# A hybrid attention layer on one core: late output weights spread over more attention units, the fourth head's inverse root on VectorE from a bit guess, the root table loaded ahead

## The chip, the core and the metric

The kernel runs on one NeuronCore of one Trainium2 chip. The time is the device time of one execution in microseconds (us). The work of the core is shared by five engines with instruction queues of their own: PE (TensorE, matmuls and transposes), DVE (VectorE), ACT (ScalarE), POOL (GpSimd) and SP, which here only starts transfers. An engine runs its instructions in the order in which they stand; engines wait for one another through semaphores.

## What is computed

One layer over 512 frames and 16 meta tokens of width 1024. The part that the change touches is the token mixer and its output projection:

```python
mu = jnp.mean(o, axis=-1, keepdims=True)                  # retention output, 4 heads of 128
var = jnp.mean(jnp.square(o - mu), axis=-1, keepdims=True)
on = (o - mu) * lax.rsqrt(var + EPS)
ret = jax.nn.silu(g) * on
...
s = jnp.where(sel_ok, q @ k_sel, NEG)                      # sparse attention, 8 heads
att = (softmax(s) @ v_sel) @ w_uv
h = h + jnp.concatenate([ret, att], axis=-1) @ w_out       # the output projection
hn = rmsnorm(h, norm_ffn)
h = h + peer(hn, ...)                                      # 16384 experts, most of the time
```

## The kernel before

The program is a row of blocks with a barrier between them: `project` (input projection and the selection of keys), `mix_rows` (retention, attention, output projection, the norm before the experts and the first two query products), `route` (top experts), `experts`. Matmuls with weights run in three passes over a high and a low part of each operand (`three_pass`), so each piece of a weight is first split: `split_hi` on ACT writes the high part, `split_lo` on POOL subtracts it from the raw weight. The 16 pieces of `w_out` (units 0 to 15 of `ws`) are split inside `mix_rows`; units 0 to 6 early, the rest at steps that the table `LATE_W` gives.

The heart of `mix_rows` is a loop `for i in range(STEPS)` that stands once for each engine. Step `i` treats attention unit `i`, which is one head of one block of 128 rows: 32 units, eight to a block, the widest block (528 keys) first, then 400, 272 and 144 keys. In a step:

- PE computes `scores(i)`, transposes the probabilities of unit `i-2` (`turn_probs`), and multiplies those of unit `i-3` with the values (`values`). At step 9 it also turns the gathered probabilities of the meta keys of the eight units of block 0 (`turn_meta(0)`), at step 11 it adds their part (`add_meta`) and then turns the finished retention columns (`turn_mixed`), which the projection needs. For this last all four heads must be gated.
- DVE computes the masked scores, their peak and the shift (`mask(i)`), and copies the transposed probabilities of unit `i-2` out of PSUM (`copy_probs`). PE's `values(i-3)` waits for that copy.
- ACT computes the exponentials of unit `i`, the high halves of the weights that `LATE_W[i]` names, and at the steps of `NORM_AT` normalizes one retention head.
- POOL copies the meta columns of unit `i`'s probabilities (`meta_probs`), then does the low halves for `LATE_W[i]`, and at the steps of `GATE_AT` multiplies a retention head with its gate. PE's `turn_meta(0)` waits for the copy of unit 7.

Retention's inverse standard deviations are made in two groups: heads 0 to 2 before the loop and head 3 inside it. For head 3 ACT takes the square root at step `LATE_ROOT` = 8, and DVE at step 9 takes the reciprocal and one Newton step (`refine_rstd`, five instructions) and the offset. The square root and the exponential stand in different function tables of ACT, so each change between them is an `ACT_TABLE_LOAD`.

After the loop ACT squares the new rows (`square`), takes their root (`ffn_sqrt`, again behind a table load), DVE refines and scales the rows, PE transposes them (`turn_normed`) and starts on the queries.

## Time and profile before

| | before |
|---|---|
| time, median of 3 runs (lowest, highest) | 1719.62 us (1718.4, 1720.39) |
| the profiled execution: its time, its span | 1721.74 us, 1719.9 us |
| PE, DVE, ACT, POOL busy, share of the span | 98%, 63%, 34%, 55% |
| granted TensorE clock over the span | 0.996 |
| `mix_rows` in the span | about 237 to 391 us |

The span runs from the first to the last instruction of the profiled execution. Times in rows are counted from its start. An instruction's row gives start, duration, engine, line, operation and tiles; what stands in square brackets is the idle time of that engine before it and who ended it.

### The profile page before, as it was taken

How to read it: one execution, taken by the hardware profiler on the slowest of the kernel's cores; microseconds unless marked ns; L12 is line 12 of the kernel's file. 1: busy time of each engine (PE TensorE's matmuls, PEld its weight loads, DVE VectorE, ACT ScalarE, POOL GpSimd, SP SyncE). 2: the span in 40 equal slices, each digit the busy share in tenths (PEclk: the TensorE clock that was granted, in tenths of full speed). 3: DMA queues.
4: the chain of work that ended last, by engine and by line, in shares of the span. 5: the costliest groups of instructions: out<-in, count | busy, mean ns of one | idle time of the engine just before them, and what ended most of it. 6: DMA issues, size and time to landing. Idle time of an engine off the chain costs nothing.

```text
span 1719.9 us, 23334 instructions
## 1 busy us (share of the span) xinstructions
PE 1689.8 (98%) x7786; PEld 1390.4 (81%) x7786; DVE 1090.5 (63%) x2933; ACT 582.0 (34%) x916; POOL 938.8 (55%) x875
## 2 busy tenths in 40 slices
PE   9999999999999999999999999999999999999997
PEld 7867877788888878888888888888888888888886
DVE  4259966455788854444444444434788888888886
ACT  4333217243323222222222222224333333333333
POOL 2744415004433027777777777762777677767710
PEclk9999999999999999999999999999999999999999
DMA  5322131026669544444447444445999999999991
GB/s 176 105 62 60 52 81 60 23 99 221 233 229 309 172 135 147 145 143 143 145 146 248 147 146 143 147 147 190 386 389 368 370 373 367 371 375 367 366 330 49
DMA packets 182673, 351.03 MB, mean 204 GB/s; under 512 B 35600, under 2 KB 118928, under 8 KB 182448
## 3 DMA queue, kind: packets, MB, share of 16 engines
q1 hardware_dynamic: 117824, 255.47, 44.5%
q0 software_dynamic: 34816, 67.41, 11.0%
q10 hardware_dynamic: 29952, 27.28, 4.8%
q8 instruction: 26, 0.43, 0.1%
q14 instruction: 55, 0.45, 0.1%
HBM read 289.04 MB, written 61.02 MB: 204 GB/s over the span
## 4 chain that ended last, share of the span: by engine, by line
PE 63%; DVE 0%; issue 0%; DVEq 0%; ACT 0%
PE psum L240 21%; PE psum L241 21%; PE psum L242 21%; DVE mixed L2135 0%; DVE mixed L2112 0%; DVEq L2059 0%; DVE rstd_final L824 0%; DVE rstd_final L828 0%; DVE rstd_final L822 0%; DVE rstd_final L826 0%; DVE rstd_final L820 0%; ACT rstd_final L2249 0%; DVE rstd_final L2121 0%; DVE rstd_final L2119 0%
## 5 line engine op out<-in xcount | busy, mean ns | idle before, releaser
L2323 POOL DMA_INDIRECT gate_map<-gate_total,gate_at x384 | 403.5, 1051 | 204.9 <-DVE same_expert L2066 114.2
L240 PE MATMUL psum<-x_hi,ts_hi_u 128*128 128x512 f32 x1024 | 399.9, 391 | 4.0 <-PEq L1681 2.2
L241 PE MATMUL psum<-x_lo,ts_hi_u 128*128 128x512 f32 x1024 | 399.1, 390 | 0.0
L242 PE MATMUL psum<-x_hi,ts_lo_u 128*128 128x512 f32 x1024 | 398.9, 390 | 0.0
L1569 DVE TENSOR_TENSOR ts_lo_u<-ts_raw_u,ts_hi_u 128x1024 fp32r<-128x1024 f32 x116 | 142.2, 1226 | 340.7 <-ACT ts_hi_u L1564 338.1
L240 PE MATMUL psum<-v_hi,c_hi 128*128 128x512 f32 x768 | 298.8, 389 | 0.0
L242 PE MATMUL psum<-v_hi,c_lo 128*128 128x512 f32 x768 | 298.8, 389 | 0.0
L241 PE MATMUL psum<-v_lo,c_hi 128*128 128x512 f32 x768 | 298.8, 389 | 0.0
L1564 ACT ACTIVATE ts_hi_u<-ts_raw_u 128x1024 fp32r<-128x1024 f32 x128 | 135.4, 1058 | 398.6 <-PE psum L242 398.6
L2226 ACT ACTIVATE v_hi<-v_raw 128x1024 fp32r<-128x1024 f32 x128 | 135.8, 1061 | 313.3 <-PE psum L242 310.2
L240 PEld LDWEIGHTS psum<-x_hi,ts_hi_u 128*128 128x128 f32 x1024 | 192.6, 188 | 44.7 <-issue 2.6
L242 PEld LDWEIGHTS psum<-x_hi,ts_lo_u 128*128 128x128 f32 x1024 | 192.7, 188 | 40.1
L2311 POOL DMA_INDIRECT sparse_rows<-in_peer_v,v_row x128 | 154.4, 1206 | 129.1 <-DVE sparse_more L2102 38.2
L241 PEld LDWEIGHTS psum<-x_lo,ts_hi_u 128*128 128x128 f32 x1024 | 192.7, 188 | 39.7
L2083 DVE TENSOR_TENSOR v_lo<-v_raw,v_hi 128x1024 fp32r<-128x1024 f32 x128 | 156.8, 1225 | 80.3 <-ACT v_hi L2226 79.9
L2317 POOL DMA_INDIRECT sparse_act<-up_acts_sparse,act_at x128 | 175.3, 1370 | 41.5 <-issue 39.8
L242 PEld LDWEIGHTS psum<-v_hi,c_lo 128*128 128x128 f32 x768 | 144.2, 188 | 30.0
L240 PEld LDWEIGHTS psum<-v_hi,c_hi 128*128 128x128 f32 x768 | 144.2, 188 | 29.8
L241 PEld LDWEIGHTS psum<-v_lo,c_hi 128*128 128x128 f32 x768 | 144.2, 188 | 29.8
L2066 DVE SCALAR_TENSOR_TENSOR same_expert<-expert,gates 128x128 f32<-128x128 f32 x384 | 111.8, 346 | 0.0
L240 PE MATMUL psum<-whi_in,h_hi 128*128 128x512 f32 (+1 forms) x280 | 109.8, 392 | 0.8 <-DVE wlo_in L280 0.8
L1600 ACT ACTIVATE ut_out_u<-psum 128x512 f32<-128x512 f32 x128 | 76.0, 594 | 95.6 <-PE psum L242 94.3
(258 smaller groups left out, 2298.2 us busy)
## 6 DMA issues: line engine op xcount, KB each, us to landing
ts_raw_u<-in_peer_u SPq DMA_DIRECT2D x128, 512.0 KB, 3.6
v_raw<-in_peer_v SPq DMA_DIRECT2D x128, 512.0 KB, 6.0
gate_map<-zeros SPq DMA_DIRECT2D x32, 768.0 KB, 6.6
act_in<-up_acts SPq DMA_DIRECT2D x128, 192.0 KB, 6.3
gate_in<-gate_map SPq DMA_DIRECT2D x128, 192.0 KB, 6.8
up_acts<-ut_out_u ACTq DMA_DIRECT2D x104, 192.0 KB, 1.9
raw_in<-in_w_in SPq DMA_DIRECT2D x56, 256.0 KB, 2.8
ts_raw_wq<-in_peer_wq SPq DMA_DIRECT2D x16, 512.0 KB, 6.3
```

The source lines that it names most:

```text
L240: nc.tensor.matmul(out, l_hi, r_hi, start=first, stop=False)
L241: nc.tensor.matmul(out, l_hi, r_lo, start=False, stop=False)
L242: return nc.tensor.matmul(out, l_lo, r_hi, start=False, stop=last)
L1564: nc.scalar.activation(self.hi[:, n % self.slots], self.raw[:, n % self.raws], ACT.Copy).then_inc(self.hi_done, 1)
L1569: eng_ops.tensor_tensor(self.lo[:, n % self.slots], self.raw[:, n % self.raws], self.hi[:, n % self.slots].bitcast(F32), ALU.subtract).the ...
L1600: nc.scalar.activation(self.out[:, i], self.bank[n % 2], ACT.Gelu).then_inc(self.bank_read, 1)
L2066: nc.vector.scalar_tensor_tensor(out=dn.same[:, j % 2], in0=expert[:, b], scalar=expert[:, b, j:j + 1], in1=gates[:, b].rearrange("p h k - ...
L2083: nc.vector.tensor_tensor(dn.v_lo[:, i], dn.v_raw[:, e % RAW], dn.v_hi[:, i].bitcast(F32), ALU.subtract).then_inc(v_lo_done, 1)
L2226: nc.scalar.activation(dn.v_hi[:, i], dn.v_raw[:, e % RAW], ACT.Copy).then_inc(v_hi_done, 1)
L2311: nc.gpsimd.indirect_dma_start(dn.rows[:, r], None, v_rows, bass.IndirectOffsetOnAxis(places["v_row"][:, j:j + 1], 0)).then_inc(row_in[r], 16)
L2317: nc.gpsimd.indirect_dma_start(dn.picked[:, j:j + 1], None, act_cells, bass.IndirectOffsetOnAxis(places["act_at"][:, j:j + 1], 0)).then_in ...
L2323: nc.gpsimd.indirect_dma_start(gate_cells, bass.IndirectOffsetOnAxis(places["gate_at"][:, b, j:j + 1], 0), dn.total[:, b, j:j + 1], None). ...
```

## The change

1. `LATE_W`: units 9 to 15 of the output weights are split at other steps. Before: 9 and 10 at step 2, then one at each of steps 3 to 7. After: one at each of steps 2, 3, 7, 8, 9, 11 and 12. ACT's high half and POOL's low half move together.
2. Head 3: ACT's square root at step 8 is gone, and with it its two table loads. DVE makes the inverse root by itself from a shift of the bits and three Newton steps: eleven instructions and the offset, twelve in all, at step 7 in place of six at step 9. `LATE_ROOT` is 6, so ACT normalizes head 3 at step 7 (before: 9) and POOL gates it at step 8 (before: 10).
3. Behind the last exponentials ACT runs one unused square root, so the table load for `ffn_sqrt` moves ahead of the squares.
4. In `experts` the loads of activations and gates of one tile signal one semaphore in place of two.

```diff
-    LATE_ROOT = DSA_HEADS
+    LATE_ROOT = DSA_HEADS - 2
     LAST_HEAD, LAST_SUMS = RET_HEADS - 1, 7
-    LATE_W = {1: (7, 8), 2: (9, 10), 3: (11,), 4: (12,), 5: (13,), 6: (14,), 7: (15,)}
+    LATE_W = {1: (7, 8), 2: (9,), 3: (10,), 7: (11,), 8: (12,), 9: (13,), 11: (14,), 12: (15,)}
     NORM_AT = {2: 0, 3: 1, 4: 2, LATE_ROOT + 1: LAST_HEAD}
     GATE_AT = {4: 0, 5: 1, 6: 2, LATE_ROOT + 2: LAST_HEAD}
+    ROOT_BITS, ROOT_STEPS = 0x5F3759DF, 3
...
+            def guessed_roots(y, v, t):
+
+                nc.vector.tensor_scalar(ab["guess"][:], v.bitcast(U32), 1, None, ALU.logical_shift_right).then_inc(guessed, 1)
+                dve.wait_ge(guessed, 1)
+                nc.vector.tensor_scalar(y.bitcast(U32), ab["guess"][:], -1.0, float(ROOT_BITS), ALU.mult, ALU.add).then_inc(guessed, 1)
+                for n in range(ROOT_STEPS):
+                    dve.wait_ge(guessed, 3 * n + 2)
+                    nc.vector.tensor_tensor(t, y, y, ALU.mult).then_inc(guessed, 1)
+                    dve.wait_ge(guessed, 3 * n + 3)
+                    nc.vector.scalar_tensor_tensor(out=t, in0=t, scalar=-0.5, in1=v, op0=ALU.mult, op1=ALU.mult).then_inc(guessed, 1)
+                    dve.wait_ge(guessed, 3 * n + 4)
+                    nc.vector.scalar_tensor_tensor(out=y, in0=t, scalar=1.5, in1=y, op0=ALU.add, op1=ALU.mult).then_inc(guessed, 1)
+                dve.wait_ge(guessed, 3 * ROOT_STEPS + 2)
+
             def inverse_roots(g):
                 hs = HEAD_GROUPS[g]
-                dve.wait_ge(root, g + 1)
-                refine_rstd(nc, dve, refined, g, rstd[:, hs], var[:, hs], ab["ret_step"][:, hs])
+                if g == 0:
+                    dve.wait_ge(root, 1)
+                    refine_rstd(nc, dve, refined, 0, rstd[:, hs], var[:, hs], ab["ret_step"][:, hs])
+                else:
+                    guessed_roots(rstd[:, LAST_HEAD], var[:, LAST_HEAD], ab["ret_step"][:, LAST_HEAD])
...
-                if i == LATE_ROOT:
-                    ret_sqrt(1)
...
+                if i == UNITS - 1:
+                    nc.scalar.activation(ab["unused"][:], ident[:, 0:1], ACT.Sqrt)
...
-                dve.wait_ge(act_in[i], 16 * use)
-                dve.wait_ge(gate_in[i], 16 * use)
+                dve.wait_ge(factors_in[i], 32 * use)
```

What stands on DVE around step 7, before: `mask(7)`, `copy_probs(5)`, `mask(8)`, `copy_probs(6)`.

```order
L1291 ISA att_masked,att_peak<-psum,sel_bias 128x528 [waits att_exp_done,att_scored]
L1291 ISA att_peak 128x1
L1295 TENSOR_SCALAR att_shift<-att_peak 128x1 [waits att_mask_done]
L1302 COPY att_probs_t<-psum 128x512 [waits att_valued,att_probs_turned]
L1291 ISA att_masked,att_peak<-psum,sel_bias 128x400 [waits att_exp_done,att_scored]
```

The same place after the change, from `mask(7)`'s shift to `copy_probs(5)` (the three rows that are repeated once more for each Newton step are shown once here).

```order
L1315 TENSOR_SCALAR att_shift<-att_peak 128x1 [waits att_mask_done]
L1282 TENSOR_SCALAR ret_guess<-ret_var 128x4
L1284 TENSOR_SCALAR ret_rstd<-ret_guess 128x4 [waits ret_root_guessed]
L1287 TENSOR_TENSOR ret_step<-ret_rstd 128x4 [waits ret_root_guessed]
L1289 SCALAR_TENSOR_TENSOR ret_step<-ret_step,ret_var 128x4 [waits ret_root_guessed]
L1291 SCALAR_TENSOR_TENSOR ret_rstd<-ret_step,ret_rstd 128x4 [waits ret_root_guessed]
...
L1301 SCALAR_TENSOR_TENSOR ret_offset<-ret_moments,ret_rstd 128x4 [waits ret_root_guessed]
L1322 COPY att_probs_t<-psum 128x512 [waits att_valued,att_probs_turned]
```

Twelve instructions now stand between the shift of unit 7 and the copy that PE's `values(5)` waits for; the six of before stood two steps later, ahead of `copy_probs(7)`.

On POOL, from the meta copy of unit 5 (first row) to those of units 8 to 10 (last row), before:

```order
L1022 COPY att_meta_probs<-att_probs 128x16 [waits att_exp_done]
L280 TENSOR_TENSOR wlo_out<-raw_out,whi_out 128x512 [waits w_hi_in]
L1011 TENSOR_TENSOR mixed<-mixed,gate 128x4x128 [waits ret_normed]
L1022 COPY att_meta_probs<-att_probs 128x16 [waits att_exp_done]
L280 TENSOR_TENSOR wlo_out<-raw_out,whi_out 128x512 [waits w_hi_in]
L1011 TENSOR_TENSOR mixed<-mixed,gate 128x4x128 [waits ret_normed]
L1022 COPY att_meta_probs<-att_probs 128x16 [waits att_exp_done]
L280 TENSOR_TENSOR wlo_out<-raw_out,whi_out 128x512 [waits w_hi_in]
L1022 COPY att_meta_probs<-att_probs 128x16 [waits att_exp_done] x3
```

The same stretch after, up to the copy of unit 9:

```order
L1025 COPY att_meta_probs<-att_probs 128x16 [waits att_exp_done]
L1014 TENSOR_TENSOR mixed<-mixed,gate 128x4x128 [waits ret_normed]
L1025 COPY att_meta_probs<-att_probs 128x16 [waits att_exp_done]
L1014 TENSOR_TENSOR mixed<-mixed,gate 128x4x128 [waits ret_normed]
L1025 COPY att_meta_probs<-att_probs 128x16 [waits att_exp_done]
L281 TENSOR_TENSOR wlo_out<-raw_out,whi_out 128x512 [waits w_hi_in]
L1025 COPY att_meta_probs<-att_probs 128x16 [waits att_exp_done]
L281 TENSOR_TENSOR wlo_out<-raw_out,whi_out 128x512 [waits w_hi_in]
L1014 TENSOR_TENSOR mixed<-mixed,gate 128x4x128 [waits ret_normed]
L1025 COPY att_meta_probs<-att_probs 128x16 [waits att_exp_done]
```

The splits are gone between the copies of units 5 and 7; the first late one (unit 11 of the weights) stands right behind the copy of unit 7, and head 3's gate behind the next.

On ACT at steps 8 and 9 the square root stood between two table loads, before:

```order
L1479 ACTIVATE att_probs,att_total<-att_masked,att_shift 128x400 [waits meta_probs_gathered,att_probs_turned,att_shift_done]
L1461 ACT_TABLE_LOAD
L1461 ACTIVATE ret_rstd<-ret_var 128x4 [waits ret_var_done]
L1479 ACT_TABLE_LOAD [waits meta_probs_gathered,att_probs_turned]
L1479 ACTIVATE att_probs,att_total<-att_masked,att_shift 128x400 [waits att_shift_done]
L1504 ACTIVATE att_meta_t<-psum 128x128 [waits meta_probs_turned]
```

After, from the split that follows unit 7's exponentials to the meta copy of step 9:

```order
L275 ACTIVATE whi_out<-raw_out 128x512 [waits w_loaded_in3]
L1489 ACTIVATE mixed<-ret_sums,ret_offset,ret_rstd 128x128 [waits ret_sums_copied,ret_offset_done]
L1489 ACTIVATE mixed<-ret_sums,ret_offset,ret_rstd 128x128 x3
L1499 ACTIVATE att_probs,att_total<-att_masked,att_shift 128x400 [waits meta_probs_gathered,att_probs_turned,att_shift_done]
L275 ACTIVATE whi_out<-raw_out 128x512 [waits w_loaded_in0]
L1499 ACTIVATE att_probs,att_total<-att_masked,att_shift 128x400 [waits meta_probs_gathered,att_probs_turned,att_shift_done]
L1522 ACTIVATE att_meta_t<-psum 128x128 [waits meta_probs_turned]
```

No table load is left in the loop. The normalization of head 3, which waits for DVE's offset, stands ahead of the exponentials of unit 8.

## Rows read from the trace of the kernel before

**Rows 1.** The page: busy time of each engine, share, number of instructions.

```profile
PE 1689.8 (98%) x7786; PEld 1390.4 (81%) x7786; DVE 1090.5 (63%) x2933; ACT 582.0 (34%) x916; POOL 938.8 (55%) x875
```

**Rows 2.** Waits of PE inside `mix_rows`: total, times, longest, in us.

```profile
PE psum L1119 <- POOL att_meta_probs L1022: 1.4, 1, 1.4
PE psum L1165 <- DVE x_lo L1368: 0.9, 1, 0.9
```

**Rows 3.** Timeline of PE, steps 8 to 11.

```profile
283.22 0.89 PE L1059 MATMUL psum<-dk_t,dq_t 128*128 128x400 f32 x2
283.95 0.60 PE L1073 MATMUL psum<-ident,att_probs 128*128 128x128 f32 x4
284.39 1.00 PE L1088 MATMUL psum<-decay_m,att_probs_t 128*128 128x64 f32 x8
285.23 0.89 PE L1059 MATMUL psum<-dk_t,dq_t 128*128 128x400 f32 x2
287.53 0.33 PE L1119 MATMUL psum<-ident,att_meta_probs 128*128 128x128 f32 x1 [1.42 <-POOL att_meta_probs L1022]
287.70 0.60 PE L1073 MATMUL psum<-ident,att_probs 128*128 128x128 f32 x4
...
291.84 1.02 PE L1123 MATMUL psum<-att_meta_w,att_meta_t 128*128 128x512 f32 x2
292.70 0.49 PE L1073 MATMUL psum<-ident,att_probs 128*128 128x128 f32 x3
293.34 0.65 PE L1139 MATMUL psum<-ident,mixed 128*128 128x128 f32 x4
```

**Rows 4.** Timeline of POOL, steps 6 and 7.

```profile
286.07 1.26 POOL L1011 TENSOR_TENSOR mixed<-mixed,gate 128x512 f32<-128x512 f32 x1
...
287.43 1.27 POOL L280 TENSOR_TENSOR wlo_out<-raw_out,whi_out 128x512 fp32r<-128x512 f32 x1
```

**Rows 5.** Timeline of DVE: unit 7's shift, and head 3's refinement at step 9.

```profile
282.90 0.15 DVE L1295 TENSOR_SCALAR att_shift<-att_peak 128x1 f32<-128x1 f32 x1
...
287.44 1.27 DVE L822 TENSOR_TENSOR ret_step<-ret_rstd 128x4 f32<-128x4 f32 x1
288.75 0.16 DVE L824 TENSOR_TENSOR ret_step<-ret_step,ret_var 128x4 f32<-128x4 f32 x1
...
289.35 0.16 DVE L1281 SCALAR_TENSOR_TENSOR ret_offset<-ret_moments,ret_rstd 128x4 f32<-128x4 f32 x1
289.43 0.69 DVE L1302 COPY att_probs_t<-psum 128x512 f32<-128x512 f32 x1
```

**Rows 6.** The tile `ret_var`: duration in ns, least, median, greatest.

```profile
L1275 DVE TENSOR_SCALAR ret_var<-ret_moments x2: 540/860/1180, 262.4 to 273.6; 128x12 f32<-128x12 f32 x1, 128x4 f32<-128x4 f32 x1
```

**Rows 7.** Timeline of ACT, steps 5, 6 and 8.

```profile
281.55 0.62 ACT L274 ACTIVATE whi_out<-raw_out 128x512 fp32r<-128x512 f32 x1
282.07 0.72 ACT L1479 ACTIVATE att_probs<-att_masked,att_shift 128x528 f32<-128x528 f32 x1
...
285.70 1.28 ACT L1461 ACT_TABLE_LOAD   x1
```

**Rows 8.** Timeline of ACT, DVE and PE behind the loop.

```profile
358.45 0.28 ACT L1504 ACTIVATE att_meta_t<-psum 128x128 f32<-128x128 f32 x1 [1.18 <-PE psum L1119]
...
364.13 0.18 DVE L820 RECIPROCAL ffn_rstd<-ffn_rstd 128x3 f32<-128x3 f32 x1 [1.15 <-ACT ffn_rstd L1446]
...
370.46 0.68 DVE L1343 TENSOR_TENSOR mixed<-psum,mixed 128x512 f32<-128x512 f32 x1
...
369.73 0.39 PE L242 MATMUL psum<-whi_out,x_lo 128*128 128x512 f32 x1
...
373.16 0.65 PE L1165 MATMUL psum<-ident,att_masked 128*128 128x128 f32 x4 [0.86 <-DVE x_lo L1368]
```

**Rows 9.** Windows: us, busy of PE, PEld, DVE, ACT, POOL, granted clock, DMA share, GB/s.

```profile
284.00:288.00 4.00, 2.58 (x19) 1.94 (x18) 2.83 (x9) 3.64 (x8) 4.00 (x6) 1.00 0.01 2
620.00:624.00 4.00, 3.49 (x8) 2.75 (x9) 1.23 (x1) 0.00 (x0) 0.00 (x0) 0.57 0.82 241
```

More of the change, by code:

```diff
@@ L182, in program @@
                 offset=sb("ret_offset", [P, RET_HEADS, NB], c=stream),
+                guess=sb("ret_guess", [P, NB], U32, c=stream),
                 ret_step=sb("ret_step", [P, RET_HEADS, NB], c=stream),
@@ L848, in mix_rows @@
     xn = [raw_rows[:, 0], raw_rows[:, 1]] + [x[:].rearrange("p r n -> p (r n)")[:, 0:D] for x in (masked, probs)]
-    tables_in = [sem(f"decay_in{h}") for h in range(RET_HEADS)]
+    tables_in = {h: sem(f"decay_in{h}") for h in range(1, RET_HEADS)}
     meta_in = sem("decay_meta_in")
@@ L864, in mix_rows @@
     offset_done = sem("ret_offset_done")
+    guessed = sem("ret_root_guessed")
     sums_copied = sem("ret_sums_copied")
@@ L1356, in refine @@
                 dve.wait_ge(ffn_root, g + 1)
-                refine_rstd(nc, dve, refined, 2 + g, rstd_f[:, ps], mean[:, ps], ab["step"][:, ps])
+                refine_rstd(nc, dve, refined, 1 + g, rstd_f[:, ps], mean[:, ps], ab["step"][:, ps])
             def scale_rows(p):
@@ L1459, in ret_sqrt @@
                 hs = HEAD_GROUPS[g]
-                act.wait_ge(var_done, g + 1)
+                act.wait_ge(var_done, 1)
                 nc.scalar.activation(rstd[:, hs], var[:, hs], ACT.Sqrt).then_inc(root, 1)
@@ L2024, in experts @@
     v_in = [sem(f"d_v_in{i}") for i in range(RAW)]
-    act_in = [sem(f"d_act_in{i}") for i in range(RAW)]
-    gate_in = [sem(f"d_gate_in{i}") for i in range(RAW)]
+    factors_in = [sem(f"d_factors_in{i}") for i in range(RAW)]
     v_hi_done = sem("v_hi_done")
@@ L2262, in load_act @@
                     sp.wait_ge(coef_done, e - RAW + 1)
-                sp.dma_start(dn.act_in[:, e % RAW], acts_d[e]).then_inc(act_in[e % RAW], 16)
+                sp.dma_start(dn.act_in[:, e % RAW], acts_d[e]).then_inc(factors_in[e % RAW], 16)
             def load_gate(e):
@@ L2268, in load_gate @@
                     sp.wait_ge(coef_done, e - RAW + 1)
-                sp.dma_start(dn.gate_in[:, e % RAW], gates_d[e]).then_inc(gate_in[e % RAW], 16)
+                sp.dma_start(dn.gate_in[:, e % RAW], gates_d[e]).then_inc(factors_in[e % RAW], 16)
             for n in range(TILES):
```

## The prediction

> **What bounds the kernel now.** I read the page first: PE is busy 98% of the span, DVE 63%, ACT 34%, POOL 55% [rows 1]. So what counts is only what makes PE wait. The list of PE's waits then shows how little there is to win in `mix_rows`: the longest wait is 1.4 us at `turn_meta(0)`, for POOL's copy of unit 7's meta columns, and behind the loop there is one of 0.9 us at `turn_normed` for the low half of the first normed rows [rows 2]. The timeline of PE shows the first in its place [rows 3]. From its starts I take what PE needs when nothing holds it: scores 0.73 us, turning four pieces 0.44 (three: 0.33), values 0.84, the meta turn 0.17, the meta product 0.86. From `values(5)` at 284.39 to `turn_mixed` these are 0.84+0.73+0.17+0.44+0.84+0.73+0.33+0.84+0.73+0.86+0.33 = 6.84, that is 291.23. It starts at 293.34, so 2.1 us are lost there, 1.57 of them ahead of the meta turn (285.96 to 287.53). The reason is on POOL: the gate of head 2 runs from 286.07 to 287.33, and the copy of unit 7 stands behind it [rows 4]. ACT's table loads, 1.28 us each [rows 7], fall into the same time, but PE's wait names POOL, not ACT.
>
> **The splits.** Three high halves of 0.52 each (start to start, 281.55 to 282.07 [rows 7]) leave ACT ahead of unit 6's exponentials, and the same low halves of 1.27 leave POOL [rows 4]. ACT then no longer lags: exponentials start when their shift is there, for unit 7 at 282.90+0.15 = 283.05 [rows 5]. They end near 283.9, gates 1 and 2 are done by then, and POOL's copy 7 ends near 284.1, two us before PE could want it (285.96). The 1.57 us go. The late splits cost nothing: PE reads the last pieces at steps 14 and 15, and the last split is at step 12; the extra 0.52 at step 11 on ACT stands ahead of the high half of the mixed rows, whose low half on DVE waits for `mask(12)` anyway. If that cover were gone it would cost 0.5. The gate of head 3, two steps earlier, also frees `turn_mixed`.
>
> **The root on DVE.** ACT loses two table loads and the root, some 2.8 us, off PE's path. DVE gets twelve dependent small instructions at step 7. One follows the other in (289.35-288.75)/3 = 0.20 us, the copy follows in 0.08 [rows 5]. They start at 282.98, directly behind unit 7's shift, and without any disturbance `copy_probs(5)` starts at 282.98+11x0.20+0.08 = 285.26 and ends 0.69 later, at 285.95. PE wants `values(5)` at 284.39 and gets it at 286.0: a new wait of 1.6 us. The trace has no row of the shift and the multiplication on U32; the nearest rows are 0.15 and 0.16, and anything down to 0.1 or up to 0.4 moves the chain by 0.4 at most.
>
> Then comes what I think decides the sign. In the trace a DVE instruction of four elements took 1.27 us: it began at 287.44, one hundredth behind a large POOL instruction that ran from 287.43 for 1.27 [rows 4, 5]. The `TENSOR_SCALAR` on `ret_var` took 0.54 and 1.18 for 4 and 12 elements, where its like take 0.16 [rows 6, 5]. I read it so that a small DVE instruction with all operands in SBUF stands until POOL's large one has ended. The Trainium skill says in "GPSIMD Engine Reference", Key points, that GpSimd shares its SBUF interfaces with VectorE, with contention for DVE instructions in a 2-port mode or with two SBUF inputs. By that rule the ten instructions with two inputs are exposed for certain, and the first two only if the mode is used; the trace agrees with it in the rows just named. It speaks against this change, which puts twelve such instructions where POOL is busy.
>
> Where is POOL? Unit 6's shift comes about one unit (2.0 to 2.2 us) ahead of unit 7's, near 280.9; its exponentials end near 281.7; copy 6 and gate 2 follow, so gate 2 runs from about 282.0 to 282.4 on for 1.26, to 283.3 to 283.7. The chain's first instructions are held by 0.3 to 0.7. Then ACT's split of unit 11 ends at 283.05+0.72+0.62 = 284.39, and POOL's low half runs from 284.44 to 285.70. The instruction of the chain that comes up then, the sixth or seventh, ends at 285.70. Five or six remain: the copy starts at 286.6 to 286.8, ends at about 287.5, and PE waits 3.0 to 3.2 us at `values(5)`. No third collision: POOL's next large instruction needs unit 8's exponentials, which stand on ACT behind head 3's normalization and so behind the chain.
>
> Queued behind the chain on DVE are `mask(8)` and `copy_probs(6)`: 0.68 (estimate from the 0.69 of the copy) and 0.69 behind 287.5, so 288.9; PE comes to `values(6)` at 287.55+0.84+0.73+0.17+0.44 = 289.7. Fine. ACT waits for the offset (286.9), normalizes head 3 in four instructions (an estimate: together under 2.0), then unit 8's exponentials (0.72), to 289.7 at the latest; PE turns them at 291.3. Fine too. So from 284.39 to `turn_mixed` PE needs 6.84 and one wait: 3.1 in place of 2.1, a loss of 1.0; without collisions 1.6 in place of 2.1, a gain of 0.5. The break-even is a chain of 2.8 us from first start to copy.
>
> **The root table ahead.** Load and unused root add 1.28 and about 0.15 ahead of the squares; ACT then waited 1.18 for `turn_meta(3)` [rows 8], so the meta copy comes 0.25 late and PE with it. In return `ffn_sqrt` has no load before it, and DVE's reciprocal, which waited 1.15 for it, comes about 0.6 earlier. But `add_rows` at 370.46 needs PE's last product (369.73+0.39 = 370.12 [rows 8]), now 370.37 plus a semaphore's 0.05: it moves by less than 0.1, and PE's wait at 373.16 depends on what follows it. Sum -0.05; bounds +0.25 (nothing given back) and -0.3 (DVE was the only reason for the 0.34 before the add).
> The Trainium skill puts a switch of tables at about 2.66 us, load and drain, in "ScalarE: Activation LUTs", What ACT_TABLE_LOAD costs. By that the meta copy would be some 1.4 later still, and the sum +1.4 here. The row shows 1.28.
>
> **One semaphore for two.** Nothing. One wait less per tile on DVE, which is off the path in `experts`: PE's list has no wait for the coefficients. The bounds are zero and zero as long as PE stays the bound.
>
> **The sum.** The changes add +1.0 and -0.05. Behind 391 us PE works without waits that hang on other times, so a shift passes through. Against its own execution, 1721.74 becomes 1722.7; that one is 2.1 above the median of 1719.62, so the median becomes 1720.6.
>
> **The rivals.**
> 1. Both collisions (forecast): +1.0, 1720.6. Chance 0.52.
> 2. One or none: -0.5 to +0.5, 1719.1 to 1720.1. For it speaks that I have only three such instructions in the trace, and that gate 2 may be through by 283. 0.32.
> 3. Slower: the wait at `values(5)` brings TensorE's clock down. The 1.4 us wait of before left it at 1.00; but at 620 to 624 it stood at 0.57 after the pause between two blocks [rows 9], which costs 4x0.43 = 1.7 us. If once down it stayed at 1.2 GHz over the sparse steps that follow, some 9 us by the steps of [rows 3], it would cost 4.5: 1725. It decides (over +3.4 in all) from 4.9 us at half clock on. 0.1, half of it over the bound.
> 4. Copy 7 stays PE's wait, because something else on POOL is late: then the splits give nothing, and the chain's wait only moves it. POOL's sum of work between copies 5 and 7 falls from 5.0 to 2.5 us in 4.4, which speaks against it. +1 to +2.5: 1721 to 1722. 0.03.
> 5. Something gives more than PE's waits there, 2.1 and 0.9: I know nothing that could. 0.03.
>
> **How the numbers follow.** What a measurement of this kernel tells from no change is about 0.2%, 3.4 us; all of rivals 1, 2 and 4 lie inside. The range takes in rival 2's best (1719.1) and most of rival 3 (1722.3 for a short fall), and 1.0 to 1.5 for the spread of medians, whose three runs of before lie 2.0 apart: 1717.6 to 1723.2. Faster 0.04, same 0.89, slower 0.07.
>
> **What would show it.** Right: PE has no wait for POOL at the meta turn; a wait of about 3 us for DVE's `att_probs_t` at `values(5)`; two of the twelve instructions last 0.5 to 1.2 us and end with a POOL instruction; no table load in the loop; `ffn_sqrt` at once, but PE's wait at `turn_normed` still 0.6 or more. Wrong: a wait under 2.1 us at `values(5)` (then the change gains), a granted clock under 1 between 284 and 300, or a shift between 391 us and the end that differs from that at 391.

## The result: 0.3% slower, and where the time went

The changed kernel takes 1725.11 us (median of 11 runs, 1722.73 to 1726.11); the kernel before took 1720.00 beside it (1717.44 to 1721.98, 11 runs). The ratio is 1.0028, 95% interval 1.0020 to 1.0037, so 3.4 to 6.4 us slower. Timed a second time, beside other runs of the kernel before, it was 1.0023 (1.0014 to 1.0032), with a median of 1723.22. I had forecast 1720.6 and a range of 1717.6 to 1723.2.

The eleven times of the first timing fall in two groups, five at 1722.7 to 1723.4 us and six at 1725.1 to 1726.1, with nothing between them; the mean granted clock of the first five is 0.996, of the six 0.994 or 0.995. The median is the lowest time of the upper group. In the second timing ten of the eleven lie at 1722.4 to 1724.0 and one at 1727.0. So how far 1725.11 lies above the forecast is in part the draw of that occasion; that the kernel is slower is not.

The waits of PE from 270 to 376 us after the change (us in total, times, longest), to be held against [rows 2]:

```profile
PE psum L1091 <- DVE att_probs_t L1322: 3.1, 1, 3.1
PE psum L1091 <- DVE mixed L1347: 1.6, 2, 0.9
PE psum L1142 <- ACT att_meta_t L1522: 1.2, 2, 0.7
PE psum L241 <- DVE x_lo L1355: 0.7, 2, 0.5
```

The wait for POOL's meta columns is gone, and a wait of 3.1 us for VectorE's copy has come, as forecast. The timeline of PE shows where it stands, and something else; it answers to [rows 3]:

```profile
286.79 1.97 PE L1091 MATMUL psum<-decay_m,att_probs_t 128*128 128x64 f32 x8 [3.08 <-DVE att_probs_t L1322]
288.55 1.65 PE L1062 MATMUL psum<-dk_t,dq_t 128*128 128x400 f32 x2
...
292.66 1.65 PE L1062 MATMUL psum<-dk_t,dq_t 128*128 128x400 f32 x2
294.10 0.85 PE L1076 MATMUL psum<-ident,att_probs 128*128 128x128 f32 x3
294.74 1.75 PE L1091 MATMUL psum<-decay_m,att_probs_t 128*128 128x64 f32 x8
296.32 0.89 PE L1062 MATMUL psum<-dk_t,dq_t 128*128 128x400 f32 x2
...
298.23 0.60 PE L1142 MATMUL psum<-ident,mixed 128*128 128x128 f32 x4
```

The same two matmuls of 128x400 take 1.65 us at 288.55 and at 292.66, and 0.89 at 296.32, as they did everywhere in [rows 3]. From the wait on, up to 296.3, PE works at half speed. Windows of the same stretch (us, busy of PE, PEld, DVE, ACT, POOL, granted clock, DMA share, GB/s) say why:

```profile
280.00:284.00 4.00, 3.71 (x25) 2.95 (x24) 3.09 (x10) 2.20 (x6) 3.34 (x6) 1.00 0.01 4
284.00:288.00 4.00, 1.21 (x6) 1.21 (x6) 3.76 (x12) 1.84 (x5) 0.93 (x1) 0.76 0.23 68
288.00:292.00 4.00, 4.00 (x16) 3.23 (x16) 1.45 (x5) 1.90 (x7) 2.86 (x4) 0.50 0.00 0
292.00:296.00 4.00, 4.00 (x17) 3.23 (x16) 1.22 (x4) 1.17 (x3) 1.35 (x3) 0.50 0.00 0
296.00:300.00 4.00, 4.00 (x23) 2.89 (x23) 2.46 (x7) 1.72 (x4) 0.95 (x3) 0.96 0.00 0
```

The granted clock is 0.50, the lower of its two levels (1.2 GHz, against 2.4), in two whole windows; in the kernel before it was 1.00 in each of these five. With the parts in the windows beside them that is 2x(0.24+0.50+0.50+0.04)x4 = 10.2 us, of which about 9.5 (from the first matmul behind the wait to 296.3) have PE at work; the rest lies in the wait. Note how little the other views tell of it: PE is called busy for 4.00 of 4.00 us there, and in the list of waits nothing but the 3.1 us stands out.

The chain of DVE in the loop (start, duration), with what POOL did beside it:

```profile
281.61 1.27 POOL L1014 TENSOR_TENSOR mixed<-mixed,gate 128x512 f32<-128x512 f32 x1
...
282.06 0.15 DVE L1315 TENSOR_SCALAR att_shift<-att_peak 128x1 f32<-128x1 f32 x1
282.13 0.77 DVE L1282 TENSOR_SCALAR ret_guess<-ret_var 128x4 uint32<-128x4 uint32 x1
...
282.93 0.17 DVE L1284 TENSOR_SCALAR ret_rstd<-ret_guess 128x4 uint32<-128x4 uint32 x1
...
283.67 1.26 POOL L281 TENSOR_TENSOR wlo_out<-raw_out,whi_out 128x512 fp32r<-128x512 f32 x1 [0.31 <-ACT whi_out L275]
283.72 1.23 DVE L1287 TENSOR_TENSOR ret_step<-ret_rstd 128x4 f32<-128x4 f32 x1
...
284.99 0.16 DVE L1289 SCALAR_TENSOR_TENSOR ret_step<-ret_step,ret_var 128x4 f32<-128x4 f32 x1
...
286.05 0.69 DVE L1322 COPY att_probs_t<-psum 128x512 f32<-128x512 f32 x1
```

Two instructions are long, 0.77 and 1.23 us, and each ends with a large one of POOL (281.61+1.27 = 282.88, 283.67+1.26 = 284.93). The other ten take 0.16 or 0.17.

**The account of the two profiled executions** (spans 1719.9 before, 1723.3 after). From the start of the mixing loop's `scores(8)` to `turn_mixed` the stretch grew from 10.12 to 15.85 us, +5.73. `scores(8)` itself began 0.84 earlier (in the fourteen executions of this document it begins between 282.38 and 283.31), the projections and attention units after it took 0.33 longer (62.33 for 62.00), the short stretches around them -0.12 in sum, and routing to experts -1.64, because the execution of before had one more short fall of the clock, at the change from `mix_rows` to `route`. The window of before shows it:

```profile
392.00:396.00 4.00, 4.00 (x11) 3.10 (x11) 0.79 (x6) 0.88 (x2) 4.00 (x3) 0.59 0.80 259
```

After the change this block change lies some 5 us later, and the clock stays up:

```profile
396.00:400.00 4.00, 3.32 (x17) 2.68 (x16) 0.97 (x6) 1.70 (x3) 3.12 (x3) 1.00 0.52 168
400.00:404.00 4.00, 4.00 (x19) 3.34 (x18) 0.00 (x0) 1.55 (x2) 3.07 (x2) 1.00 1.00 396
```

Such falls at the block changes come and go between executions of one kernel: the changed kernel's second profiled execution has one here (0.86 at 392 to 396, 0.72 at 396 to 400), its first has none. So I count them as no part of the change. The rest sums to +5.73+0.33-0.12 = +5.94 for this execution; less the 0.84 and 1.64 that is the 3.4 between the spans.

### The profile page after: what moved, and what is told of

Read it like the earlier page. It is cut to its first block, busy times and chain, and to the rows that moved or that the text cites. A ratio compares the mean times of both kernels' runs of the same rounds, so it can differ in the third digit from the quotient of the medians.

```text
span 1723.3 us, 23335 instructions
## 1 busy us (share of the span) xinstructions
PE 1692.3 (98%) x7786; PEld 1393.4 (81%) x7786; DVE 1092.9 (63%) x2939; ACT 579.4 (34%) x914; POOL 937.9 (54%) x875
## 4 chain that ended last, share of the span: by engine, by line
PE 63%; DVE 0%; issue 0%; DVEq 0%; ACT 0%
PE psum L241 21%; PE psum L242 21%; PE psum L243 21%; DVE mixed L2153 0%; DVE mixed L2130 0%; DVEq L2078 0%; DVE rstd_final L825 0%; DVE rstd_final L829 0%; DVE rstd_final L823 0%; DVE rstd_final L827 0%; DVE rstd_final L821 0%; ACT rstd_final L2267 0%; DVE rstd_final L2139 0%; DVE rstd_final L2137 0%
```

## Experiments

"Stretch" is the time from `scores(8)` to `turn_mixed` in the profiled execution; "at half clock" is worked out from its 4 us windows as above. Each kernel was timed in 11 runs (root only in 5) beside the kernel before, on four occasions with medians of before of 1720.00, 1719.23, 1719.90 and 1720.02. Compare kernels by the ratio, not by the median. A ratio is known to about 0.0009 either way, 1.5 us, so most neighbours in the table are told apart by the stretch of one profiled execution and not by the times.

| kernel | PE's wait at `values(5)` | stretch | at half clock | median | ratio to before (95%) |
|---|---|---|---|---|---|
| before | none (1.4 at the meta turn) | 10.12 | 0 | 1720.0 | |
| changed | 3.1 | 15.85 | 10.2 | 1725.11 | 1.0028 (1.0020 to 1.0037) |
| splits only | 0 (1.6 at `values(7)`) | 10.88 | 0 | 1719.86 | 1.0005 (0.9996 to 1.0014) |
| root only | 5.8 | 16.43 | 6.9 | 1727.47 | 1.0054 (1.0040 to 1.0068) |
| filled wait | filled | 11.32 | 0 | 1720.83 | 1.0011 (1.0002 to 1.0020) |
| half filled | 1.7 | 12.98 | 3.4 | 1721.64 | 1.0013 (1.0004 to 1.0022) |
| spread root | 0.7 | 9.87 | 0 | 1720.00 | 1.0004 (0.9995 to 1.0013) |
| guess tile behind | 3.1 | 12.94 | 3.4 | 1721.91 | 1.0011 (1.0002 to 1.0020) |
| POOL kept free | 1.4 | 11.26 | 3.4 | 1721.29 | 1.0010 (1.0001 to 1.0019) |
| POOL free, chain longer | 2.5 | 13.72 | 6.8 | 1722.37 | 1.0014 (1.0005 to 1.0023) |
| spread and reordered | 0 | 7.93 | 0 | 1716.92 | 0.9982 (0.9973 to 0.9991) |
| changed, again | 3.1 | 12.92 | 3.4 | 1723.22 | 1.0023 (1.0014 to 1.0032) |
| guess tile padded | 3.1 | 14.50 | 6.8 | 1723.30 | 1.0024 (1.0015 to 1.0033) |
| tile only | none (1.4 at the meta turn) | 10.11 | 0 | 1719.75 | 1.0002 (0.9993 to 1.0011) |

My theory after the result: the wait of DVE's chain is what I had computed, and it costs +1.2; the rest is TensorE's clock, which falls in the wait or right behind it. The rivals: the chain and its collisions cost more than the wait shows, or another part of the change (the splits, the table, the new tile) does.

**The splits alone.** The kernel before with the new table.

```diff
-    LATE_W = {1: (7, 8), 2: (9, 10), 3: (11,), 4: (12,), 5: (13,), 6: (14,), 7: (15,)}
+    LATE_W = {1: (7, 8), 2: (9,), 3: (10,), 7: (11,), 8: (12,), 9: (13,), 11: (14,), 12: (15,)}
```

Expected:

> The kernel before with the new table of weight splits alone; root on ACT at step 8 as before, no root table ahead. Theory A (the changed kernel loses by its DVE chain at step 7: a wait of 3.1 us, then 9 us of PE at half clock): this part alone gains. PE's 1.4 us wait at turn_meta(0) goes, granted clock stays 1.00 between 284 and 300, turn_mixed starts 1.6 to 2.1 us earlier against the scores of step 8; time 1.5 to 2.5 below before. Rival B (it is the moved splits that hurt, through ACT or POOL work beside the projection): time above before by 1 or more.

The gain did not come. The meta turn's wait went, and two others took its place (PE's waits, the two that are new):

```profile
PE psum L1088 <- DVE att_probs_t L1302: 1.6, 1, 1.6
...
PE psum L1139 <- POOL mixed L1011: 1.0, 1, 1.0
```

The first is head 3's refinement at step 9, which now meets a low half that came later; the second is head 3's gate, late behind another of them:

```profile
287.66 1.25 DVE L826 TENSOR_SCALAR ret_step<-ret_step 128x4 f32<-128x4 f32 x1
```

```profile
287.62 1.27 POOL L280 TENSOR_TENSOR wlo_out<-raw_out,whi_out 128x512 fp32r<-128x512 f32 x1 [1.86 <-ACT whi_out L274]
...
292.61 1.27 POOL L1011 TENSOR_TENSOR mixed<-mixed,gate 128x512 f32<-128x512 f32 x1
```

So the splits remove nothing by themselves: they move POOL's work to where the next user meets it. They cost no fall of the clock. The stretch is 0.76 longer than before; the ratio agrees with that, and also with no difference at all.

**The root alone.** The changed kernel with the old table and without the root table ahead.

```diff
-    LATE_W = {1: (7, 8), 2: (9,), 3: (10,), 7: (11,), 8: (12,), 9: (13,), 11: (14,), 12: (15,)}
+    LATE_W = {1: (7, 8), 2: (9, 10), 3: (11,), 4: (12,), 5: (13,), 6: (14,), 7: (15,)}
...
-                if i == UNITS - 1:
-                    nc.scalar.activation(ab["unused"][:], ident[:, 0:1], ACT.Sqrt)
```

> The changed kernel with the old table of splits and no root table ahead: DVE makes head 3's inverse root at step 7, all else as before. Theory A: PE waits about 3 us at values(5) for att_probs_t, the granted clock falls to about 0.5 from some 287 on; time 3 to 6 above before, as the whole change or more. Rival B: within 1 of before.

With POOL's large instructions close together, five of the chain's twelve are held, and PE waits 5.8 us, where I had expected 3. The time is 8.2 us above before, more than the 3 to 6 expected; as expected the clock falls, for 6.9 us. Four of the five:

```profile
283.55 1.20 DVE L1284 TENSOR_SCALAR ret_rstd<-ret_guess 128x4 uint32<-128x4 uint32 x1
...
284.99 1.11 DVE L1289 SCALAR_TENSOR_TENSOR ret_step<-ret_step,ret_var 128x4 f32<-128x4 f32 x1
286.13 1.18 DVE L1291 SCALAR_TENSOR_TENSOR ret_rstd<-ret_step,ret_rstd 128x4 f32<-128x4 f32 x1
...
287.55 1.12 DVE L1289 SCALAR_TENSOR_TENSOR ret_step<-ret_step,ret_var 128x4 f32<-128x4 f32 x1
```

POOL beside them, one piece after the other:

```profile
283.45 1.27 POOL L1014 TENSOR_TENSOR mixed<-mixed,gate 128x512 f32<-128x512 f32 x1
...
284.82 1.25 POOL L281 TENSOR_TENSOR wlo_out<-raw_out,whi_out 128x512 fp32r<-128x512 f32 x1
286.04 1.25 POOL L1014 TENSOR_TENSOR mixed<-mixed,gate 128x512 f32<-128x512 f32 x1
...
287.40 1.25 POOL L281 TENSOR_TENSOR wlo_out<-raw_out,whi_out 128x512 fp32r<-128x512 f32 x1
```

Each long DVE instruction ends within 0.05 us of a POOL one, whichever of the forms it is. So the split's spread is worth some 2.7 us of wait to this root, though nothing to the kernel of before. The execution also prices the root table ahead, which it lacks: with it, in the changed kernel, the stretch from `turn_meta(3)` to the first `turn_normed` is 0.13 longer (11.99 for 11.86), and the one from there to the routing 0.22 shorter (21.63 for 21.85). That is -0.09 in sum, from one execution each.

**The wait filled.** The changed kernel, with 13 matmuls on PE whose results nobody reads, ahead of `values(5)`.

```diff
+                if i == LATE_ROOT + 2:
+                    pe.wait_ge(meta_w_done, 1)
+                    for _ in range(13):
+                        nc.tensor.matmul(psum[:, T_BANK, :], ws.hi[:, 0, 0:P], ws.hi[:, 1], start=True, stop=True)
                 if 3 <= i < UNITS + 3 and not opens_block(i - 3):
```

> The changed kernel with 13 unneeded matmuls (128x512, about 0.23 us each at full clock, 3.0 in all) on PE just ahead of values(5), into a PSUM bank that nobody reads then: PE has the same wait for the copy, but works through it. Theory A: the granted clock stays at 1.00 from 284 to 300, the wait at values(5) shrinks to under 0.4, values(5) starts where it starts in the changed kernel, and the time falls by 3.5 to 5 against it, to about 1 above before or less. Rival C (the clock falls there because of the sparse attention matmuls, whatever the wait): clock still about 0.5, time as the changed kernel.

This decides between the theories. DVE's chain and its collisions are the same (0.77 and 1.27), PE gets its operands no earlier (`values(5)` starts 4.45 us behind `scores(8)`, 4.41 in the changed kernel), and it has more to do. Yet the stretch is 11.32 instead of 15.85. PE's timeline has the dummies in the place of the wait, and the following matmuls at full speed:

```profile
284.39 3.23 PE L1234 MATMUL psum<-whi_out 128*128 128x512 f32 x13
287.76 1.10 PE L1091 MATMUL psum<-decay_m,att_probs_t 128*128 128x64 f32 x8
288.70 0.89 PE L1062 MATMUL psum<-dk_t,dq_t 128*128 128x400 f32 x2
```

The window view of the whole stretch gives the clock, 1.00:

```profile
284.00:300.00 16.00, 15.34 (x87) 11.93 (x86) 11.00 (x35) 8.40 (x22) 8.68 (x12) 1.00 0.05 17
```

So the wait as such costs 11.32-10.12 = +1.2 us against before (forecast +1.0), and the fall of the clock 15.85-11.32 = 4.5 us in the changed kernel's execution. Rivals that look for these 4.5 us in the chain, in ACT or in the tile fall by this: all of these are in the filled kernel too. The times say the same less sharply: the filled kernel's interval (1.0002 to 1.0020) touches that of the changed kernel's first timing and overlaps that of the second.

**Half of the wait filled.** Six dummies instead of thirteen.

> The changed kernel with 6 instead of 13 dummy 128x512 matmuls ahead of the values product of unit 5: they fill about 1.5 us of the 3.1 us wait, the rest (about 1.5 us) stays a wait; the results of the dummies are not read. Question: must the whole wait be filled? Theory that a wait of this length at this place already brings the clock down (as 1.4 us did with VectorE's chain undisturbed): half clock for 3 to 6 us, 1722 to 1724. Rival, that what counts is the work in the stretch as a whole: clock 1.00 and the stretch from scores(8) to the mixed transposes 11.3 us, as with 13 dummies, 1720.8.

PE then waits 1.7 us, and the clock falls again, for 3.4 us; the stretch is 12.98, 1.7 over the filled one. In this execution filling a part did not do; the ratios (1.0013 and 1.0011) do not tell the two kernels apart.

```profile
288.00:292.00 4.00, 4.00 (x20) 3.23 (x19) 1.93 (x5) 2.49 (x8) 2.71 (x4) 0.58 0.00 0
```

**POOL kept free beside the chain.** The changed kernel, with gate 2 three steps later and the weight halves 11 to 13 one step later.

```diff
-    LATE_W = {1: (7, 8), 2: (9,), 3: (10,), 7: (11,), 8: (12,), 9: (13,), 11: (14,), 12: (15,)}
+    LATE_W = {1: (7, 8), 2: (9,), 3: (10,), 8: (11,), 9: (12,), 10: (13,), 11: (14,), 12: (15,)}
-    GATE_AT = {4: 0, 5: 1, 6: 2, LATE_ROOT + 2: LAST_HEAD}
+    GATE_AT = {4: 0, 5: 1, 9: 2, LATE_ROOT + 2: LAST_HEAD}
```

> The changed kernel with POOL's large instructions moved out of the time of the DVE chain (gate of head 2 to step 9, weight units 11 to 13 one step later). Theory A (two collisions with POOL lengthen the chain by 1.6 us and so the wait to 3.1): none of the twelve instructions lasts over 0.3 us, PE waits 1.5 to 1.7 at values(5), the granted clock stays 1.00, from scores of step 8 to turn_mixed 9.5 to 10 us against 15.85 in the changed kernel and 10.12 before; time 4 to 6 below the changed kernel. Rival E (the long small instructions are DVE's own, not POOL's doing): they stay long, and so does the wait.

The first half came out: no instruction of the chain is long, from the first to the copy it takes 2.24 us (11 pitches of 0.20 and 0.08), and PE waits 1.4.

```profile
282.70 0.16 DVE L1282 TENSOR_SCALAR ret_guess<-ret_var 128x4 uint32<-128x4 uint32 x1
...
284.94 0.69 DVE L1322 COPY att_probs_t<-psum 128x512 f32<-128x512 f32 x1
```

This shows by intervention what the rows of before only suggested: take POOL's large instruction away and the long small ones are gone. The Trainium skill has it in "SBUF — State Buffer", SBUF: two separate sides: an exclusive lock for the whole instruction, not a split of bandwidth. The trace of the changed kernel agrees for an instruction with two inputs in SBUF: 1.23 for a `TENSOR_TENSOR` that otherwise takes 0.16. For the held `TENSOR_SCALAR` (0.77), which has one, the page has the lock only in a 2-port mode, and no run here shows which mode it ran in.

The second half did not. I had expected a clock of 1.00 and a stretch of 9.5 to 10; it is 11.26, because the clock fell here too (and the time is 1.0010 of before, 3.8 below the changed kernel's first median and 1.9 below its second, for an expected 4 to 6):

```profile
284.00:288.00 4.00, 2.59 (x14) 1.59 (x13) 2.72 (x11) 2.78 (x7) 0.28 (x2) 0.84 0.01 2
288.00:292.00 4.00, 4.00 (x25) 3.66 (x23) 2.06 (x7) 1.40 (x4) 4.00 (x5) 0.73 0.18 66
```

PE is busy for 2.59 of 4 us at 284 to 288 here, and was for 2.58 in the kernel before [rows 9], at a clock of 1.00. A wait of 1.4 us at `values(5)` brought the clock down, one of 1.4 us at the meta turn, one values and one scores product (1.6 us) later, did not. My idea that a wait of this length is harmless, taken from before, was wrong. Here the fall came behind the wait: the `values(5)` that ended it ran at full speed (1.10 us), and the scores after it took 1.55 instead of 0.89.

**The same, with a longer chain.** Five more small instructions at the chain's end, on data that nobody reads.

```diff
-                dve.wait_ge(guessed, 3 * ROOT_STEPS + 2)
+                for _ in range(5):
+                    dve.wait_ge(guessed, 3 * ROOT_STEPS + 2)
+                    nc.vector.tensor_tensor(t, y, v, ALU.mult).then_inc(extra, 1)
+                    dve.wait_ge(extra, _ + 1)
```

> As e6_free_pool with five more unneeded four-element instructions behind the chain, 0.2 us each: the wait at values(5) is about 2.6 us, without any collision. Theory A, first form (any wait of more than about 2.5 us here brings the clock down): granted clock about 0.5 from some 287 on, scores of step 8 to turn_mixed 14 to 15.5, time as the changed kernel. Second form (it takes the whole 3.1): clock 1.00, stretch about 10.6, time 1 above e6_free_pool.

PE waits 2.5, as computed, and is at half clock for 6.8 us. So the wait of 2.5 us brings the clock down, as the first form said, but the stretch is 13.72, under the 14 to 15.5 expected. The median, 1722.37, is 1.1 over the kernel without the five, which their intervals do not tell from nothing.

**The root spread over four steps.** Three of the twelve instructions at each of the steps 4 to 7, behind `copy_probs`, so that no copy waits for more than three.

```diff
+    ROOT_FROM, PER_STEP = 4, 3
...
+                if 0 <= i - ROOT_FROM < 12 // PER_STEP:
+                    root_part(i - ROOT_FROM)
...
-                if i == LATE_ROOT + 1:
-                    inverse_roots(1)
```

> The changed kernel with the same twelve DVE instructions three to a step at steps 4 to 7, each behind copy_probs, in place of all at step 7 ahead of it; head 3 normalized at step 8, gated at 9. Theory A: no wait at values(5) over 0.5, clock 1.00, time 1 to 2.5 below before. Rival D (the shared access of DVE and POOL is what costs, wherever the instructions stand): two or more collisions of 0.5 to 1.2 us appear and PE waits for att_probs_t at some step, time above before.

PE waits 0.7 for the copy (one of the three was held for 1.13 by gate 2) and 0.8 for head 3's gate, which stands behind weight halves on POOL. Rival D's collisions are there too: besides the 1.13, two more of the twelve lasted 0.58 and 0.47, but PE did not wait for them. No fall of the clock, stretch 9.87, and a time like that of before, where I had expected 1 to 2.5 less. So the root on VectorE is not what costs; where its twelve instructions stand is.

**The guess tile behind the weights.** The changed kernel with the 16-byte tile allocated last.

```diff
-                guess=sb("ret_guess", [P, NB], U32, c=stream),
...
             ws_out = WeightStream(stream, "out", sem, sb)
+            ab["guess"] = sb("ret_guess", [P, NB], U32, c=stream)
```

> The changed kernel, only the 16 byte tile ret_guess is placed in SBUF behind the weight tiles in place of ahead of them. Theory A about the 0.3 us that all kernels with this tile lost between the first projection and turn_meta(3) (62.3 in place of 62.0 to 62.1 us): the tile shifts the weights of the projection by 16 bytes and each matmul that reads them gets a hair slower; then this stretch goes back to 62.0 to 62.1 and all else stays, time 0.3 below the changed kernel, which the times cannot tell. Rival: the moved splits or the root do it; the stretch stays at 62.3.

The projections and attention units behind the stretch are back at 62.01 us from 62.33, as expected. The time, though, was 3 us lower than the changed kernel's, and the clock was down for 3.4 us instead of 10.2. That called for the next three.

**The changed kernel again, a padded tile, the tile alone.** Nothing changed; the tile 64 bytes long at its old place; and the kernel before with the unused tile.

```diff
-                guess=sb("ret_guess", [P, NB], U32, c=stream),
+                guess=sb("ret_guess", [P, 4 * NB], U32, c=stream),
```

> The changed kernel once more, beside the three that follow, on one chip. Question: is the difference of some 3 us between the changed kernel and the same one with the 16-byte guess tile behind the weights (1721.9 against 1725.1, half clock for 3.4 us instead of 9.5 us, other numbers alike) a property of the kernels, or of the occasion on which they were timed? Theory that the kernels differ: 1724 to 1726 again, half clock for about 9 us after the wait of 3.1 us. Rival, that the length of the fall is drawn by the occasion (same instructions, another phase of whatever grants the clock): a median anywhere between 1721.5 and 1725.

> The changed kernel with the guess tile at its old place ahead of the output weights, but 64 bytes long instead of 16, so that all tiles behind it keep their alignment to 64 bytes of the kernel before. Theory that the 0.3 us over the projections is alignment: the stretch from the first projection to the last attention unit is 62.0 us, as with the tile behind the weights. Rival, that any shift of the weights costs it: 62.3. Time: by the theory that the tile also sets the length of the fall, 1721.9 as with the tile behind the weights; else as the changed kernel less 0.3.

> The kernel before plus an unused tile of 16 bytes ahead of the output weights, nothing else. It prices the placement by itself. Theory: the stretch from the first projection to the last attention unit goes from 62.0 to 62.3 us, everything else stays, total +0.3 (1720.2 beside a before of 1719.9). Rival: the placement costs only together with other edits: 62.0 and +0.0.

The same kernel, with the same wait of 3.1, had the clock down for 3.4 us this time, and a median of 1723.22:

```profile
288.00:292.00 4.00, 4.00 (x22) 3.55 (x21) 2.16 (x6) 3.05 (x9) 2.47 (x3) 0.63 0.00 0
292.00:296.00 4.00, 4.00 (x21) 2.79 (x21) 2.12 (x9) 0.90 (x3) 1.78 (x4) 0.94 0.00 0
```

So the length of the fall is not fixed by the kernel: four executions with the same wait of 3.1 us (changed, again, tile behind, tile padded) had 10.2, 3.4, 3.4 and 6.8 us at half clock, and stretches 4.5, 1.6, 1.6 and 3.2 us over the filled one. That is a little under half of the time at the lower clock. Where the fall begins differs as well: in the first execution it lay partly in the wait (`values(5)` took 1.97 us), in the second it came after it (1.10). The theory that this kernel always takes 1724 to 1726 fell.

The tile is a cost of its own: alone in the kernel before it takes the time from the first projection to the last attention unit from 62.00 to 62.31. The other traces agree: 62.30 to 62.34 in all nine executions with 16 bytes ahead of the weights, 62.00 to 62.07 in the four without the tile or with it behind. Its total, 1.0002 (0.9993 to 1.0011), can't tell 0.3 us from nothing. The padded tile leaves it at 62.24, so a shift by 64 bytes costs nearly as much as one by 16, and alignment to 64 bytes is not the main reason. The third product of each projection shows it in its mean, after the change and with the tile behind the weights, 301 to 356 us:

```profile
L243 PE MATMUL psum<-whi_out,x_lo 128*128 128x512 f32 x40 | 15.9, 397 | 0.0
```

```profile
L243 PE MATMUL psum<-whi_out,x_lo 128*128 128x512 f32 x41 | 16.1, 394 | 0.0
```

**The version that beats both.** The spread root, with gate 2 out of its way (at step 8), the halves from 12 on later, and the tile behind the weights. The cut shows the two tables alone.

```diff
-    LATE_W = {1: (7, 8), 2: (9,), 3: (10,), 7: (11,), 8: (12,), 9: (13,), 11: (14,), 12: (15,)}
+    LATE_W = {1: (7, 8), 2: (9,), 3: (10,), 7: (11,), 10: (12,), 11: (13,), 12: (14,), 13: (15,)}
-    GATE_AT = {4: 0, 5: 1, 6: 2, LATE_ROOT + 2: LAST_HEAD}
+    GATE_AT = {4: 0, 5: 1, 8: 2, LATE_ROOT + 2: LAST_HEAD}
```

> The spread chain of e4_spread with the two waits that were left in it taken away: gate of head 2 from step 6 to 8 (it collided with the chain), weight units 12 to 15 at steps 10 to 13 so that head 3's gate at step 9 stands ahead of them, and ret_guess behind the weights. Theory A: no wait of PE over 0.3 between steps 8 and 11, the stretch from scores of step 8 to turn_mixed 8.0 to 8.8 us (PE's own work is 8.0), clock 1.00, time 1.5 to 2.5 below before. Rival: what is won there comes back as a new wait for the late weights at steps 13 to 15, or is lost in the differences that the clock makes at the block changes.

1716.92 us, 0.9982 of before (0.9973 to 0.9991). The stretch is 7.93 us, the 2.1 us that PE lost there in the kernel before are all back, and no wait above 0.3 is left in it. Two of the twelve instructions are still held by gates (0.58 and 0.47); they stand behind the copies, and PE does not notice. The window in which the clock of the changed kernel began to fall:

```profile
284.00:288.00 4.00, 4.00 (x31) 3.32 (x29) 3.21 (x12) 3.54 (x10) 2.86 (x4) 1.00 0.15 45
```

## Why the prediction was wrong

**The splits: half right.** PE's wait for copy 7 went, at no cost at steps 8 to 12. That they gain 1.57 by themselves is not so: alone they cost 0.76, because head 3's refinement, still at step 9, then met a moved half, and its gate stood behind another. In the changed kernel the root is elsewhere, and the sum stood.

**The root on DVE: right, by mechanism and by size.** Pitch 0.20; two held instructions; the copy at 286.05, 3.92 after the chain's start, where I had 3.6 to 3.8 from 282.98 on; the wait 3.1 of 3.0 to 3.2. One detail differs: the second collision met the sixth instruction for its full length (1.23), and the first held the very first for 0.77 in place of 0.3 to 0.7. The wait's net price was +1.2 (forecast +1.0).

**The table ahead: right, as far as one execution each can tell.** -0.09 for a forecast of -0.05. ACT's `ACT_TABLE_LOAD` behind the loop took 1.28 us (361.19), PE's wait for the meta copy was 0.53 in place of 0.35, and the wait at `turn_normed` was the 0.6 that I had named. The single semaphore was not tried by itself; PE's waits name the coefficients in neither trace.

**Left out: the tile.** The change also allocates `ret_guess`, 16 bytes ahead of the output weights, which its list of four points does not name. That this could cost anything stands nowhere in the sum. It is +0.3.

**The step that failed: the clock.** The sum prices the new wait of 3.1 us at its length alone and has no term for TensorE's clock, and a granted clock under 1 between 284 and 300, which the prediction named as a sign of being wrong, is what came. "The 1.4 us wait of before left it at 1.00" was the evidence on which rival 3 got 0.10, and half of that over the bound. The evidence was one wait at one place. In all eight profiled executions with a wait of 1.4 us or more at `values(5)` (1.4, 1.7, 2.5, 3.1 four times, 5.8) the clock fell; in the one with 0.7 there, in the three with a wait of 1.4 or 1.6 at another place of the stretch, and in the one with the wait filled it did not. So the forecast should have been the wait's price plus a fall's, for which the row at 620 to 624 [rows 9] and the steps of [rows 3] already gave 1.7 to 4.5: 1722.3 to 1725. My own rival had the mechanism, the place and the 4.5; measured it was 1.6 to 4.5 for the same wait. Added up over before that is 1.2 for the wait, 0.3 for the tile, -0.1 for the table and 1.6 or 4.5 for the clock, 3.0 or 5.9; the two groups of the first timing lie some 3 and 5.5 above before. Only one execution of each timing has a trace, so that the groups are the short and the long fall is likely and not shown. The worked sum was right for the work and wrong for the speed at which it is done.

The Trainium skill has the pattern in "TensorE: Matmul & The Clock Gate", HAM oscillation: a kernel whose matmul bursts are parted by waits can pay the low clock anew after each. Here one wait was enough. I had not weighed that section against this change.

**What stays open.** What sets how long the clock stays down after one and the same wait (3.4 to 10.2 us), and why 1.4 us at `values(5)` brings it down and 1.4 us at the meta turn, two products later, doesn't: the first comes from one execution, the second from two. Also open: why a tile of 16 or 64 bytes ahead of the weights slows the projections. The two timings of the changed kernel, 1.0028 and 1.0023, agree within their intervals; the tile-behind kernel's 1.0011 lies lower than 0.3 us would make it and only just overlaps the second, and I did not settle whether that is more than chance.

## What to carry to other kernels

Where the tensor engine is the bound, price a new wait twice: once as the time until its operand comes, and once for what the lower clock would cost over the work behind it. Look in windows for the granted clock, which a busy share doesn't show, and don't take one harmless wait elsewhere as evidence. A chain of small VectorE instructions belongs behind the copy that TensorE waits for, a few at a time, and not beside large GpSimd instructions: a small one that meets a large one lasts until that one has ended. And moving GpSimd's work out of one reader's way puts it into the next one's; list who runs beside it at its new place before counting the gain.

## What the runs showed of the hardware that I had not expected

- The clock fell at a wait of 1.4 us and at one of 1.7, and it was at 1.2 GHz for 3.4, 6.8 or 10.2 us at the same wait of 3.1 us, in a stretch where PE was called busy throughout.
- Every form of DVE's small instructions was held by POOL's large one, those with one tensor operand as well (0.77 and 1.20 us for a `TENSOR_SCALAR` of four elements, 0.16 or 0.17 otherwise).
- 13 useless matmuls on the critical engine made the stretch 4.5 us shorter (11.32 for 15.85; 1.6 against the execution with the short fall, 12.92). The ratios to before are 1.0011 with them, 1.0028 and 1.0023 without.
- A tile of 16 bytes ahead of the weight tiles costs 0.3 us in 62 over the projections that read them and the attention units between them.
